# First attention of a two-block model: key panel first, compression links between attention steps, half-height masks and scores, two modulation vectors summed on GpSimd

## The chip, the cores and the metric

The kernel runs on one core of one Trainium2 chip. The metric is the device time of one execution in microseconds (us); three executions of the kernel before are shown below. TensorE is called PE, its weight loads PEld, VectorE DVE, ScalarE ACT, GpSimd POOL and SyncE SP. "The first attention" is the attention of the first layer; the times in this document are counted from the first instruction of the profiled execution.

## The reference, cut to what matters

A sequence of 256 tokens of width 1024 passes through four layers. Layer 0 is the one that is changed most:

```
mod = silu(c) @ ada_w[i] + ada_b[i]            # 6 vectors of 1024 per layer, 24 in all
h   = rms_norm(x, attn_norm) * (1 + sc) + sh
mq, mk, mv, nq, nkv, ng = split(h @ w_in)       # 512, 512, 512, 512, 768, 24 columns
o_moba = causal attention of 8 heads (64 wide) on norm+rope(mq), norm+rope(mk), mv
kc, vc = compress(kv[0,0]), compress(kv[0,1])   # 15 blocks of 32 tokens: silu(blocks @ w1) @ w2
o_nsa  = g0 * softmax(q kc) vc + g1 * causal attention(q, ks, vs) + g2 * causal attention(q, kw, vw)
x = x + g_a * (concat(o_moba, o_nsa) @ w_out);  x = x + g_f * swiglu(...)
```

With 256 tokens the selected blocks and the window of the reference cover every earlier token, so that all three of its full branches are plain causal attentions. Layer 1 has a causal attention with two maps per head, layer 2 a pooling, layer 3 a joint attention.

## The kernel before

**Projections.** Float32 products are made of three passes over a high and a low part: `L1508` (high weights, high activations), `L1509`, `L1510`. A weight arrives in units of two rows of 128 (a buffer `wraw` of four units, queue SP). ACT copies a unit to its high part `whi` (L526), DVE subtracts it to get the low part `wlo` (L903), and PE then multiplies; the split of unit u + 2 may start when unit u is done. `row_segment` does four such units and leaves a panel of rows in PSUM, which `panel_rows` copies to `work` (L597 on ACT, L955 on DVE). The projection of layer 0 is three panels in the order in0_0 (mq, mk; 1024 columns), in0_1 (mv, nq; 1024 columns), in0_2 (nkv and the gates; 792 columns). `head_norm` and `rotate` (L1059 to L1096, DVE) norm and rotate the heads of a panel while the next is multiplied; those of in0_2 have no next panel.

**Modulation vectors.** A vector of 1024 needs four ring units of 1 MB (two buffers `ring`, issued by ACT, L315). `vector_unit` multiplies each on PE (L1480: weights are columns of `cpad`, 32 wide, at four column positions), `vector_out` adds the bias on DVE (L866). `ada_step` places them between other work. Vectors 0 to 2 stand before and in in0_0, 3 and 4 in the compression, 5 in the first four attention steps. A vector is not needed before its norm or gate: 3 and 4 by the norm after out0, for which `columns(0, 1)` turns them.

**Between projection and attention.** `turns(0)` transposes 20 groups of heads (PE L1673, copies L655 on ACT and L1104 on DVE), DVE builds the compression's blocks (L1281), PE multiplies them with the compression weights (L1794, these too come through the ring), and a chain of small links follows: silu, transpose (L1800), second product (L1807, L1810), spreading (L1818), scores (L1825), softmax on DVE (L1299 to L1315), transpose (L1832), values (L1837), rows (L1319). PE, DVE and ACT take turns in it.

**Attention.** `attention(0)` has 12 steps of two heads. In step i PE does the scores of i, the transposes of i - 1 (L1723) and the values of i - 2 (L1742 to L1744); DVE takes the maxima of i (L1119 to L1121) and the rows of i - 2 (L1144 to L1163); ACT does the exponentials of i (L676) and copies the transposes of i - 1 (L690). For each head PE writes the causal mask as a product with the identity (L1705, 128 rows) and adds three score products of 64 rows (L1706 to L1708). `attention(1)` of layer 1 uses the same `scores`. Then come `out_turn(0)` (L1766), the output projection out0, the residual, the norm, and up0, whose first instruction is L1568.

The order on each engine is the order of its program; nothing is reordered by a scheduler. Waits are on semaphores, and an engine that waits holds everything behind it.

Of the kernel before, what the change touches and what calls it, by code (L numbers as in the profile page):

```python
# [7 lines left out]
F32 = mybir.dt.float32  # L8
# [7 lines left out]
P = 128  # L16
# [26 lines left out]
def shape_constants():  # L43
# [10 lines left out]
    put("causal", np.concatenate([causal, causal], 1))  # L54
# [37 lines left out]
def build(nc, x, c, positions, ada_w, ada_b, attn_norm, ffn_norm, ffn_w_gate, ffn_w_up, ffn_w_down,  # L92
# [6 lines left out]
    with stack:  # L99
# [25 lines left out]
        ident_r = sb("ident_r", [P, P], F32R)  # L125
        causal_r = sb("causal_r", [P, 2 * P], F32R)
# [26 lines left out]
        kcs = sb("kcs", [P, 32])  # L153
# [17 lines left out]
        T_BANKS = (6, 0, 1, 3)  # L171
        xn = wk(12288, 2048).rearrange("p (t n) -> p t n", t=TT)
# [8 lines left out]
        cmp_s = wk(14384, 256).rearrange("p (t h n) -> p t h n", t=TT, h=8)  # L181
        cmp_T = wk(14640, 256).rearrange("p (t n) -> p t n", t=TT)
        hidr = work[0:64, 14896:15152]
# [23 lines left out]
        for n, (a, b) in enumerate(((0, 1024), (1024, 2048), (2048, SP_IN))):  # L207
            seg(f"in0_{n}", "row", [SPI[:, :, a:b]], 4, b - a)
# [43 lines left out]

        tile0_done, quarter_done = sem("tile0_done"), sem("quarter_done")
# [15 lines left out]
        CMP_AT = 12  # L269
        RING_UNITS = 4 * VECTORS + 4  # L270
# [4 lines left out]
        def ring_at(g, j):  # L275

            return 4 * g + j + (0 if g < 3 else 4)

        def ring_unit(r):

            if CMP_AT <= r < CMP_AT + 4:
                return "cmp", (r - CMP_AT) // 2, (r - CMP_AT) % 2
            r -= 4 if r >= CMP_AT + 4 else 0
            return "ada", r // 4, r % 4


        STEP_PLAN = [g_ for g_ in range(VECTORS) if g_ < 6 or 9 <= g_ < 12 or g_ >= 21]
        STREAM_PLAN = {"up0": (6, 3), "up1": (12, 5), "down1": (17, 1), "up21": (18, 3)}
        EARLY = range(2, 8)
# [8 lines left out]
        def ring_dma(eng, r):  # L298
# [3 lines left out]
            kind, a, b = ring_unit(r)  # L302
# [4 lines left out]
            if kind == "ada":  # L307
                l, v = a // 6, a % 6
                at = v * D
                src = adaw[l][2 * b * P:(2 * b + 2) * P, :].rearrange("(k p) n -> p k n", p=P)[:, :, at:at + D]  # L310
                dst = dst.rearrange("p (k n) -> p k n", k=2)
            else:
                dst = dst.rearrange("p (k e) -> p k e", k=8)
                src = w1c[a][:, b * 8:(b + 1) * 8, :]
# [17 lines left out]
        PANEL_SEGS = ["in0_0", "in0_1", "in0_2", "out0", "down0", "in1_0", "in1_1", "in1_2", "out1", "down1",  # L332
# [15 lines left out]
        def q_groups(stage):  # L348

            if stage == 0:  # L350
# [7 lines left out]
                return [([src(r, t) for r in (2 * g, 2 * g + 1) for t in range(TT)], qt0[:, 2 * g:2 * g + 2, :]) for g in range(10)]  # L358
# [12 lines left out]
        def att(stage):  # L371
# [9 lines left out]
            a.ada = {0: 4, 1: 8, 3: 8}[stage]  # L381
# [14 lines left out]
        HEADS = [(0, 0), (0, 1), (0, 2), (1, 0), (1, 1), (3, 0), (3, 1), (3, 2)]  # L396
        head_squares = sem("head_squares")

        def heads_of(layer, n):

            if layer == 0:
# [7 lines left out]
                return views, HD, [wk(7728 + 1024 * t, 1024) for t in range(TT)], gains[:, lo:hi, :], n  # L409
# [16 lines left out]
        def _(sp):  # L426
# [14 lines left out]
            def weight_dma(s_, i):  # L441
                u = s_["base"] + i
                slot = u % 4
                if u >= 4:
                    sp.wait_ge(lo_ready, 2 * (u - 3))
                dst = wraw[:, slot, 0:unit_width(s_)].rearrange("p (k n) -> p k n", k=unit_split(s_))
                sp.dma_start(dst, unit_source(s_, i)).then_inc(raw_full[slot], 16)

            sp.wait_ge(ring_used, 4)
            for s_ in segs:  # L450
                if s_["name"] == "in0_1":
# [15 lines left out]
                    sp.dma_start(res[:, 1, :, :], ctx_2[0].rearrange("(t p) n -> p t n", p=P)).then_inc(sem("ctx_landed"), 16)  # L467
                for i in range(s_["count"]):
                    weight_dma(s_, i)
# [1467 lines left out]
```

## Time and profile before

| | |
|---|---|
| time of the three runs | 1750.68 us median (1749.74 to 1754.14) |
| span of the profiled execution | 1748.3 us, 2.4 us under the median; no other time of that execution is recorded |
| PE busy | 1575.0 us (90%) |
| PE weight loads busy | 1322.1 us (76%) |
| DVE busy | 940.4 us (54%) |
| ACT busy | 718.2 us (41%) |
| POOL busy | 0.2 us, 4 instructions |
| granted PE clock, mean | 0.940 |
| ACT split L526, mean of one | 1045 ns, two to a unit |
| DVE split L903, mean of one | 1216 ns, two to a unit |

The busy share of PE is an average over stages. In the stretches of in0 and of the attention steps PE is nearly always busy; between them it is not, and there its granted clock is lower as well. A stage is read by who waits for whom at its end.

### The profile page before, as it was taken

The numbers are of one execution on the slowest core, as the hardware profiler recorded it, in microseconds if no ns is written. First come the engines' busy times: TensorE is split into PE (matmuls) and PEld (weight loads), VectorE is DVE, ScalarE is ACT, GpSimd is POOL, SyncE is SP. The second block draws the span as 40 slices with busy tenths as digits, with TensorE's granted clock in tenths as the row PEclk, the third lists the DMA queues.
The fourth block names the chain that finished last, engine by engine and source line by source line (L and its number), as shares of the span: only waits on it lengthen the run. The fifth ranks groups of instructions, "written<-read, shape, count | busy, mean of one in ns | idle before, by whom it ended". The sixth has DMA issues, their size and how long they took to land.

```text
span 1748.3 us, 24466 instructions
## 1 busy us (share of the span) xinstructions
PE 1575.0 (90%) x10302; PEld 1322.1 (76%) x10302; DVE 940.4 (54%) x1610; ACT 718.2 (41%) x1098; POOL 0.2 (0%) x4
## 2 busy tenths in 40 slices
PE   3966988999989888999988999889999795999997
PEld 1753677999868657999768998679987673779986
DVE  2591346434577776433566345663355786364455
ACT  1441244334445434333335554354544443345543
POOL 0000000000000000000000000000000000000000
PEclk9988798999989889999988999889999897989999
DMA  9844602985545546998753645549755353436452
GB/s 359 313 149 158 224 19 79 315 286 188 174 147 185 176 142 214 307 307 302 242 180 97 190 172 193 181 137 300 249 185 202 109 181 109 162 129 192 169 192 85
DMA packets 165845, 336.42 MB, mean 192 GB/s; under 512 B 8160, under 2 KB 109160, under 8 KB 165480
## 3 DMA queue, kind: packets, MB, share of 16 engines
q1 hardware_dynamic: 134720, 226.71, 38.0%
q10 hardware_dynamic: 31016, 108.16, 18.2%
q8 instruction: 81, 1.33, 0.3%
q14 instruction: 28, 0.23, 0.0%
HBM read 333.79 MB, written 1.05 MB: 192 GB/s over the span
## 4 chain that ended last, share of the span: by engine, by line
PE 80%; DVE 13%; DMA 2%; ACT 2%; issue 1%; ACTq 0%; SPq 0%; DVEq 0%
PE ps L1508 21%; PE ps L1509 21%; PE ps L1510 20%; PE ps L1480 5%; DVE wlo L903 3%; PE ps L1639 2%; DVE res L981 1%; DVE work L979 1%; PE ps L1636 1%; PE ps L1723 1%; PE ps L1673 1%; PE ps L1706 1%; DMA ring<-in_ada_w_dram 1%; PE ps L1702 1%; DVE work L1066 1%
## 5 line engine op out<-in xcount | busy, mean ns | idle before, releaser
L903 DVE TENSOR_TENSOR wlo<-wraw,whi 128x1024 fp32r<-128x1024 f32 (+1 forms) x424 | 497.9, 1216 | 404.4 <-ACT whi L526 403.9
L526 ACT ACTIVATE whi<-wraw 128x1024 fp32r<-128x1024 f32 (+1 forms) x424 | 423.1, 1045 | 468.7 <-PE ps L1510 447.0
L1508 PE MATMUL ps<-hT_hi,whi 128*128 128x256 f32 x1472 | 422.5, 287 | 0.0
L1509 PE MATMUL ps<-hT_lo,whi 128*128 128x256 f32 x1472 | 416.9, 283 | 0.0
L1510 PE MATMUL ps<-hT_hi,wlo 128*128 128x256 f32 x1472 | 416.5, 283 | 0.0
L1508 PEld LDWEIGHTS ps<-hT_hi,whi 128*128 128x128 f32 x1472 | 282.7, 192 | 20.3 <-issue 18.1
L1509 PEld LDWEIGHTS ps<-hT_lo,whi 128*128 128x128 f32 x1472 | 282.9, 192 | 0.0
L1510 PEld LDWEIGHTS ps<-hT_hi,wlo 128*128 128x128 f32 x1472 | 282.8, 192 | 0.0
L1508 PE MATMUL ps<-whi,act_hi 128*128 128x512 f32 x560 | 219.0, 391 | 0.0
L1509 PE MATMUL ps<-wlo,act_hi 128*128 128x512 f32 x560 | 218.1, 390 | 0.0
L1510 PE MATMUL ps<-whi,act_lo 128*128 128x512 f32 x560 | 217.9, 389 | 0.0
L1508 PE MATMUL ps<-whi,hT_hi 128*128 128x512 f32 (+2 forms) x416 | 161.8, 389 | 7.8 <-DVE hT_lo L1030 7.4
L1509 PE MATMUL ps<-wlo,hT_hi 128*128 128x512 f32 (+2 forms) x416 | 158.9, 382 | 0.0
L1510 PE MATMUL ps<-whi,hT_lo 128*128 128x512 f32 (+2 forms) x416 | 158.2, 380 | 0.0
L897 DVE TENSOR_TENSOR act_lo<-work,act_hi 128x512 fp32r<-128x512 f32 x70 | 48.4, 692 | 191.8 <-ACT whi L526 191.8
L1508 PEld LDWEIGHTS ps<-whi,act_hi 128*128 128x128 f32 x560 | 105.1, 188 | 25.6 <-issue 3.8
L522 ACT ACTIVATE act_hi<-work 128x512 fp32r<-128x512 f32 x70 | 44.1, 630 | 191.4 <-issue 170.2
L1510 PEld LDWEIGHTS ps<-whi,act_lo 128*128 128x128 f32 x560 | 105.1, 188 | 21.9
L1509 PEld LDWEIGHTS ps<-wlo,act_hi 128*128 128x128 f32 x560 | 105.1, 188 | 21.6
L1480 PE MATMUL ps<-ring,cpad 128*32 128x256 f32 x1440 | 103.4, 408 | 11.0 <-DMA ring<-in_ada_w_dram 10.3
L1508 PEld LDWEIGHTS ps<-whi,hT_hi 128*128 128x128 f32 x416 | 79.5, 191 | 28.7 <-DVE hT_lo L1030 8.3
L1510 PEld LDWEIGHTS ps<-whi,hT_lo 128*128 128x128 f32 x416 | 79.2, 190 | 15.1
(200 smaller groups left out, 1372.1 us busy)
## 6 DMA issues: line engine op xcount, KB each, us to landing
wraw<-in_mlp_w_dram SPq DMA_DIRECT2D x96, 1024.0 KB, 5.3
ring<-in_ada_w_dram ACTq DMA_DIRECT2D x90, 1024.0 KB, 5.3
wraw<-in_ffn_w_gate_dram SPq DMA_DIRECT2D x22, 1024.0 KB, 6.4
wraw<-in_ffn_w_up_dram SPq DMA_DIRECT2D x22, 1024.0 KB, 5.6
wraw<-in_ffn_w_down_dram SPq DMA_DIRECT2D x22, 1024.0 KB, 4.9
wraw<-in_diff_w_in_dram SPq DMA_DIRECT2D x12, 1024.0 KB, 4.9
wraw<-in_attn_w_qkv_dram SPq DMA_DIRECT2D x12, 1024.0 KB, 5.1
wraw<-in_sp_w_in_dram SPq DMA_DIRECT2D x8, 1024.0 KB, 13.0
```

The lines of the kernel that those rows point to most:

```text
L522: nc.scalar.activation(act_hi[:, u % 2, :], hid[:, at:at + 512], ACT.Copy)
L526: nc.scalar.activation(whi[:, u % 2, part], wraw[:, u % 4, part], ACT.Copy).then_inc(hi_ready, 1)
L897: nc.vector.tensor_tensor(act_lo[:, u % 2, :], hid[:, at:at + 512], act_hi[:, u % 2, :].bitcast(F32), ALU.subtract)
L903: nc.vector.tensor_tensor(wlo[:, u % 2, part], wraw[:, u % 4, part], whi[:, u % 2, part].bitcast(F32), ALU.subtract).then_inc(lo_ready, 1)
L979: nc.vector.tensor_tensor(tmp[:, t, cols], ps[:, D_BANKS[q], :], gate_b[:, cols], ALU.mult).then_inc(dve_emptied, 1)
L981: nc.vector.tensor_tensor(res[:, strm, t, cols], res[:, strm, t, cols], tmp[:, t, cols], ALU.add).then_inc(sem("res_ready"), 1)
L1066: return nc.vector.tensor_tensor(views[t], views[t], g.rearrange("p a (c d) -> p a c d", c=1).to_broadcast([P, a, b, width]), ALU.mult)
L1480: ins = mm(ps[32 * c_:32 * c_ + 32, ADA_BANK, 0:256], cpad[:, 0 if g < 12 else 1, kt, :], ring_view(r)[:, kk * D + 256 * c_:kk * D + 256 * ...
L1508: mm(dst, s_hi, m_hi, start=start, stop=False, skip_group_check=skip)
L1509: mm(dst, s_hi, m_lo, start=False, stop=False, skip_group_check=skip)
L1510: return mm(dst, s_lo, m_hi, start=False, stop=stop, skip_group_check=skip)
L1639: ins = nc.tensor.transpose(ps[:, T_BANKS[b], (k % 2) * S + t * P:(k % 2) * S + (t + 1) * P], xn[:, t, k * P:(k + 1) * P], ident)
```

## The change

Four things are changed, all before up0 except the score order in layer 1.

1. **Panel order.** in0_2 is multiplied first, then in0_0, then in0_1. Key heads are normed during in0_0, MoBA heads during in0_1, and only the eight NSA query heads after the last panel. The splits of the first two units of out0 move from the end of in0 into attention steps 8 and 10 (`own=True`).
2. **Compression links.** The compression weights come through `wraw` on the SP queue, their products alternate between two column positions, and the links from the first transpose on stand one by one behind attention steps 0 to 12, in PSUM bank 7. `ada_step` leaves the compression and the attention.
3. **Scores.** The mask is two products of 64 rows per head, and masks and scores alternate between the two heads, whose operands lie in partitions 0 to 63 and 64 to 127. In layer 0 and layer 1.
4. **POOL.** Vectors 3 and 4 are summed by POOL: per ring unit two row blocks, each multiplied by a column of `cpad` and added up (30 instructions of 128x1024), and PE only folds the 128 partitions (`sum_fold`). Vector 5 stands in out0. The load of `ctx_2` moves behind the eighth unit of up0, since its buffer holds the sums.

```diff
@@ scores(i), PE, stages 0 and 1
-                        mm(ps[:, bank, 0:256], ident_r[:, :], causal_r[:, :], start=True, stop=False, skip_group_check=True)
-                        mm(ps[:, bank, 0:128], q[:, 0:128], k[:, 0:128], start=False, stop=True, skip_group_check=True)
...
+                        for half in range(2):
+                            for m in range(2):
+                                lo, hi = HD * m, HD * m + HD
+                                bank = 2 * (i % 2) + m
+                                mm(ps[:, bank, 0:256], half_r[lo:hi, HD - HD * half:3 * HD - HD * half], causal_r[lo:hi, half, :, :].rearrange("p b n -> p (b n)"),
+                                   start=(half == 0), stop=False, skip_group_check=True)
+                        for tq, tk, at in ((0, 0, 0), (1, 1, 128), (1, 0, 256)):
+                            for m in range(2):
...
+                                ins = mm(ps[:, bank, at:at + P], q[:, tq * P:(tq + 1) * P], k[:, tk * P:(tk + 1) * P], start=False, stop=True, skip_group_check=True)
@@ PE, main program
-            for n in range(3):
-                row_segment(f"in0_{n}", ada=(n == 0))
+            row_segment("in0_2", ada=True)
+            row_segment("in0_0")
+            row_segment("in0_1")
+            pe.wait_ge(sem("doubled"), 1)
+            turns(0, 0, 4)
+            pe.wait_ge(sem("moba_heads0"), 1)
+            turns(0, 4, 8)
             gate()
...
+            attention(0, beside=compression)
+            pe.wait_ge(sem("cmp_taken"), 2)
+            sum_fold(0)
+            out_turn(0)
+            sum_fold(1)
+            row_segment("out0", ada=True)
             columns(0, 1, 6)
-            out_turn(0)
-            row_segment("out0")
@@ DVE, main program
+            row_segment("in0_1", heads=lambda i: heads0(0, (i,)), own=True)
+            nc.vector.memset(mark[:, 1:2], 0.0).then_inc(sem("moba_heads0"), 1)
+            panel_rows(r0, 1024, 1024)
+            turns(0, 0, 4)
...
+            heads0(1, (0, 1))
+            turns(0, 4, 6)
+            heads0(1, (2,))
+            turns(0, 6, 8)
+            heads0(1, (3,))
+            nc.vector.memset(mark[:, 1:2], 0.0).then_inc(sem("query_heads0"), 1)
@@ ACT, beside the panels and the steps
+            def summed_ring(i):
+                if i % 2:
+                    ring_fill(ring_at(3, 0) + 2 + (i + 1) // 2)
...
+                if i in (8, 10):
+                    split_unit(by_name["out0"]["base"] + (i - 8) // 2)
@@ POOL, new
+            def row_sum(g, acc):
+                for j in range(4):
+                    r = ring_at(g, j)
+                    ring_wait(pool, r)
+                    for kk in range(2):
...
+                            link(nc.gpsimd.tensor_scalar(w, w, cpad[:, 0, kt, 0:1], None, ALU.mult))
+                            ins = nc.gpsimd.tensor_tensor(acc, acc, w, ALU.add)
...
+                    ins.then_inc(ring_used, 1)
```

PE, from the end of the projection to the first attention step; `cst` holds the identity, L1480 is a modulation unit. Before:

```order
L1659 MATMUL ps<-modrow,cst 128x256 x4
L1673 MATMUL ps<-cst,work 128x128 x40
L1794 MATMUL ps<-ring,work 30x256 x32
L1480 MATMUL ps<-ring,cpad 32x256 x8
L1800 MATMUL ps<-cst,work 128x64 x2
L1480 MATMUL ps<-ring,cpad 32x256 x8
L1807 MATMUL ps<-hbuf,w2k 128x30 x2
L1810 MATMUL ps<-w2v,hbuf 15x64 x4
L1480 MATMUL ps<-ring,cpad 32x256 x8
L1818 MATMUL ps<-vcr,cst 128x64 x8
```

The same place now; L1863 are the half masks and L1869 the scores of the first step:

```order
L1826 MATMUL ps<-cst,work 128x128 x32
L1807 MATMUL ps<-modrow,cst 128x256 x4
L1958 MATMUL ps<-wraw,work 30x256 x32
L1826 MATMUL ps<-cst,work 128x128 x8
L1863 MATMUL ps<-causal_r,half_r 128x256 x4
L1869 MATMUL ps<-work 128x128 x6
L1969 MATMUL ps<-cst,work 128x64 x2
L1863 MATMUL ps<-causal_r,half_r 128x256 x4
```

Eight of ten transpose groups stand before the compression product, two behind it, then the steps begin at once; the links are between them.

DVE, behind the last panel of the projection, now: the panel's copy (L1017), the turns' copies (L1166), the blocks of the compression (L1355), then the norm of the query heads:

```order
L1340 MEMSET mark 128x1
L1017 COPY work<-ps 128x512 x2
L1166 COPY work<-ps 128x512 x2
L1355 TENSOR_TENSOR work<-work,paramT 64x8x15 x16
L1357 MEMSET work 64x256
L1358 MEMSET work 128x256
L1121 TENSOR_REDUCE stat<-work 128x8 x2
L1136 TENSOR_SCALAR stat<-stat 128x16
```

Before, this norm stood between the panels, and that of the key heads in its place, ahead of all transposes.

POOL, new, one ring unit of vector 3 (`res` is the sum):

```order
L1567 TENSOR_SCALAR res<-ring,cpad 128x1024
L1569 TENSOR_SCALAR ring<-ring,cpad 128x1024
L1570 TENSOR_TENSOR res<-res,ring 128x1024
L1569 TENSOR_SCALAR ring<-ring,cpad 128x1024
L1570 TENSOR_TENSOR res<-res,ring 128x1024
```

Each addition is a read of two operands in SBUF, as is DVE's split L903.

## Rows read from the trace of the kernel before

**Rows 1.** Windows: start:end, length, busy us (instructions) per engine, clock, DMA.
```profile
112.00:198.00 86.00, 53.55 (x316) 30.47 (x315) 31.94 (x100) 14.97 (x30) 0.00 (x0) 0.70 0.47 160
175.00:198.00 23.00, 19.87 (x135) 10.90 (x135) 6.84 (x20) 1.70 (x2) 0.00 (x0) 0.54 0.67 229
220.00:250.00 30.00, 30.00 (x226) 26.51 (x224) 16.27 (x57) 16.79 (x64) 0.00 (x0) 1.00 0.02 8
```
**Rows 2.** Waits of PE from 40 to 262 us: total, times, longest.
```profile
PE ps L1673 <- ACT work L744: 10.6, 1, 10.6
PE ps L1480 <- DMA ring<-in_ada_w_dram: 10.3, 4, 5.4
PE ps L1794 <- DVE work L1281: 5.7, 1, 5.7
```
**Rows 3.** Timeline of PE, projection: start, duration, engine, line, operands.
```profile
45.36 0.80 PE L1508 MATMUL ps<-whi,hT_hi 128*128 128x512 f32 x1 [7.02 <-DVE hT_lo L1030]
52.80 1.07 PE L1480 MATMUL ps<-ring,cpad 128*32 128x256 f32 x16
59.51 1.07 PE L1480 MATMUL ps<-ring,cpad 128*32 128x256 f32 x16
94.59 0.39 PE L1508 MATMUL ps<-whi,hT_hi 128*128 128x512 f32 x1
95.27 0.29 PE L1508 MATMUL ps<-whi,hT_hi 128*128 128x280 f32 x1
95.65 0.39 PE L1508 MATMUL ps<-whi,hT_hi 128*128 128x512 f32 x1
112.65 0.29 PE L1510 MATMUL ps<-whi,hT_lo 128*128 128x280 f32 x1
```
**Rows 4.** Timeline of DVE, projection and behind it.
```profile
82.56 2.34 DVE L1059 TENSOR_REDUCE stat<-work 128x16 f32<-128x1024 f32 x2 [0.58 <-ACT work L575]
85.46 2.36 DVE L903 TENSOR_TENSOR wlo<-wraw,whi 128x1024 fp32r<-128x1024 f32 x2 [0.56 <-ACT whi L526]
87.74 0.17 DVE L1074 TENSOR_SCALAR stat<-stat 128x32 f32<-128x32 f32 x1
90.50 1.23 DVE L1063 TENSOR_TENSOR work<-work,rstat 128x1024 f32<-128x1024 f32 x1
137.21 4.59 DVE L1281 TENSOR_TENSOR work<-work,paramT 64x120 f32<-64x120 f32 x16
```
**Rows 5.** Timeline of PE, one attention step of layer 0 and the next step's start.
```profile
224.58 0.36 PE L1705 MATMUL ps<-causal_r,ident_r 128*128 128x256 f32 x1
226.91 0.87 PE L1723 MATMUL ps<-cst,work 128*128 128x128 f32 x6
228.88 0.36 PE L1705 MATMUL ps<-causal_r,ident_r 128*128 128x256 f32 x1
```
**Rows 6.** Timelines of DVE and ACT in that step.
```profile
227.02 0.43 DVE L1119 TENSOR_REDUCE rowmax<-ps 128x2 f32<-128x256 f32 x1 [1.51 <-PE ps L1708]
228.28 0.37 ACT L676 ACTIVATE work<-ps,rowmax 128x128 f32<-128x128 f32 x1 [1.88 <-DVE rowmax L1121]
229.11 0.18 DVE L1144 RECIPROCAL coef<-rowsum 128x4 f32<-128x4 f32 x1 [0.86 <-PE ps L1744]
229.88 0.82 ACT L690 ACTIVATE work<-ps 128x768 f32<-128x768 f32 x1
230.04 0.49 DVE L1163 TENSOR_TENSOR work<-work,hbuf 128x128 f32<-128x128 f32 x2
```
**Rows 7.** Timeline of PE, compression and modulation, in order of time.
```profile
142.05 8.38 PE L1794 MATMUL ps<-ring,work 128*30 128x256 f32 x32 [5.67 <-DVE work L1281]
174.35 3.67 PE L1818 MATMUL ps<-vcr,cst 15*128 15x64 f32 x16
```
**Rows 8.** Timeline of PE behind the attention.
```profile
260.99 1.12 PE L1497 MATMUL ps<-cst,modrow 128*128 128x128 f32 x4 [1.58 <-DVE work L1163]
297.92 0.57 PE L1568 MATMUL ps<-zero 1*128 1x512 bf16 x1
```
**Rows 9.** Waits of DVE in layer 1's attention, 603 to 622 us.
```profile
DVE rowmax L1119 <- PE ps L1708: 1.9, 4, 0.9
```

More of the change, by code:

```diff
@@ L746, in _ @@
+            row_segment("in0_1", heads=(0, 0), beside=doubled_keys, own=True)
+            panel_rows(r0, 1024, 1024)
+            next_panel()
+            turns(0, 0, 2)
+            square_heads(0, 1)
+            turns(0, 2, 8)
             gate()
-            turns(0)
-            c0 = CMP_AT
-            ring_fill(c0 + 4)
-            act.wait_ge(ring_used, c0 + 4)
+            act.wait_ge(cmp_used, 2)
             act.wait_ge(sem("hidr_zero"), 1)
             for s_ in range(2):
-                ins = nc.scalar.activation(hidr[32 * s_:32 * s_ + 30, :], ps[32 * s_:32 * s_ + 30, 0, 0:256], ACT.Silu)
+                ins = nc.scalar.activation(hidr[32 * s_:32 * s_ + 30, :], ps[32 * s_:32 * s_ + 30, LINK_BANK, 0:256], ACT.Silu)
@@ L1097, in rotate, with turns @@
                 link(ins)
-            def turns(stage):
-                for g, (_, dst) in enumerate(q_groups(stage)):
+            def turns(stage, first=0, last=None):
+                for g, (_, dst) in list(enumerate(q_groups(stage)))[first:last]:
                     if g % 2 == 1:
@@ L1323, in _ @@
+            attention(0, beside=compression)
+            vector_out(3)
+            out_turn(0)
+            vector_out(4)
+            row_segment("out0", ada=True)
+            residual(0)
             columns(0, 1)
-            out_turn(0)
-            row_segment("out0")
-            residual(0)
             norm()
@@ L1665, in gate, with turns @@
                     gate_out[0] = (gate_copied, 2 * sum(1 for g in GATES[:e + 1] if not (g[0] == 2 and g[2] == 0)))
-            def turns(stage):
-                for g, (srcs, _) in enumerate(q_groups(stage)):
+            def turns(stage, first=0, last=None):
+                groups = q_groups(stage)
+                last = len(groups) if last is None else last
+                for g in range(first, last):
+                    srcs, _ = groups[g]
                     if g >= 4:
@@ L1842, in _ @@
+            attention(0, beside=compression)
+            pe.wait_ge(sem("cmp_taken"), 2)
+            sum_fold(0)
+            out_turn(0)
+            sum_fold(1)
+            row_segment("out0", ada=True)
             columns(0, 1, 6)
-            out_turn(0)
-            row_segment("out0")
             gate()
```

494 lines of the change are left out of this document (297 added, 197 removed).

## The prediction

> **What bounds the kernel now.** I read the windows by stage first. In the attention steps PE is busy all of the 30 us at full clock, but in the 86 us between the last panel (112 us) and the first step (198 us) it is busy 53.6 us at a mean clock of 0.70, and at 0.54 in the last 23 us [rows 1]. Then the waits of PE: 10.6 us for the doubled keys behind the last head norm, 10.3 us for four ring units, 5.7 us for the blocks [rows 2]. Third, the timelines. The projection runs from 45.4 to 112.9 us [rows 3]. An attention step is 4.30 us (224.58 to 228.88), all PE: 2.33 for masks and scores (to 226.91), 1.97 for transposes and values [rows 5]. So the stretch of links is bound by latency, and the steps by PE. From the attention's last row (260.9) to up0 (297.9) are 37.0 us [rows 8]. I therefore sum the way to up0, and treat the rest as unchanged but for layer 1.
>
> **Projection.** One group of three matmuls costs 0.68 us 512 wide and 0.38 us 280 wide (94.59, 95.27, 95.65) [rows 3]. A 1024 unit has eight wide groups, 5.44 us; a 792 unit four of each, 4.24 us. The first unit cost 7.44 us (45.36 to 52.80), 2.0 over that, and a modulation unit between adds 1.27 (59.51 - 52.80 - 5.44) [rows 3]. The narrow panel is first now, so a unit lands and is split sooner: splits are proportional to width, (1 - 792/1024) x (1.05 + 2.36) = 0.8 us, and about 1 us I estimate for the landing of 0.2 MB less. Start 45.4 - 1.8 = 43.6. in0_2: 4 x 4.24 + 2.0 + 3 x 1.27 = 22.8, to 66.4. in0_0 and in0_1: 8 x 5.44 = 43.5, to 109.9. The panels in sum are the same work; 3 us come from the start and from a stall-free end. The ring needs 1 MB more often here (every 5.5 us beside 0.8 MB of weights); I leave up to 3 us for that in the range.
>
> **What DVE has left when in0_1 ends.** In in0_1 it splits unit 2 and 3 and norms 32 heads. in0_1 starts at 88.1; the split of its unit 2 opens when unit 0 is done: 93.6, plus 1.05 ACT and 2.36 DVE, 97.0; the two totals 2.34, 99.4. Unit 3 opens at 99.0 and is split at 102.4; the chain of small ones until L1063 took 2.76 (87.74 to 90.50) [rows 4], then four passes of 1.2 and a rotation of 2.8: 112.8. So DVE is 2.9 us behind PE even alone.
>
> **POOL's price.** No POOL arithmetic is in the trace. One of its 128x1024 instructions costs at least what DVE needs, 1.18 us (half of 2.36), and at most what the dearest row per element gives: 16 adds of 120 elements in 4.59 us are 2.4 ns an element, so 2.45 us [rows 4]. I take 1.7: 30 of them are 51 us, spread by the ring from 65 to about 160 us; PE wants the sums at 207 and later. Hidden, unless an instruction costs over about 4.5 us. What is not hidden is that DVE may have to wait for POOL. Before, POOL is idle, so the trace excludes neither nothing nor everything: the eight instructions of the ring units that land around 100 and 105 us fall on the head norms of in0_1, where each microsecond of DVE is on the path: 0 to 14 us. I take 6, somewhat under half, since the totals, copies and PSUM operations between read one SBUF operand.
> The Trainium skill, SBUF — State Buffer, section Who interferes with whom, says that a DVE instruction with two SBUF inputs and a GpSimd one that reads SBUF exclude each other for a whole instruction. By that rule alone, with every POOL instruction in the way, the term would be 14 us instead of 6. The Trainium skill, GPSIMD Engine Reference, section Elementwise — side-by-side cycle accounting, gives 4497 ns for an addition of 2048 elements, from which I estimate 2.2 us for 1024. No run here shows either yet.
>
> **From there to the first step.** DVE starts at 112.8 + 6 = 118.8: panel copies 1.3, turns' copies with a wait 2.1, blocks 4.6 [rows 4], two fills 0.5, query heads (half as wide: totals 1.3, chain 2.6, four passes 2.8, rotation 2.0), two copies 1.4, gates 0.7, last turns 1.1: 20.4 us. PE's own way fits under it if the 32 compression products, now at two column positions, run in pairs: each is two passes, of 0.22 to 0.26 us (8.38 us for 32 passes) [rows 7], so the 64 passes are 14 to 16 us one after the other and 7 to 8 in pairs. That column positions overlap the trace shows: L1480, 16 passes at four positions, takes 1.07 us [rows 3], where 16 in series at 0.22 would take 3.5. So the first step starts at 139.2 instead of 197.6.
>
> **The steps.** PE's part for masks and scores can fall from 2.33 to 0.9 us if the 64-row products of two heads overlap, and stay near 2.1 if they don't (then only the changes between 128 and 64 rows go). I take 1.5. But then PE is not the bound: maxima to exponentials 1.26 (227.02 to 228.28), exponentials 1.60 (to 229.88), row operations until 1.42 after 229.11 [rows 6]: a step would be 3.4 to 3.6 us. Into this go the links: on PE some 6 us (spreading L1818 3.67 at half clock is 1.8 [rows 7]), in steps 1 to 3 each with a round trip PE to DVE and back, in steps 4 and 5 1.5 and 2.0 us of softmax ahead of the next maxima, in 8 and 10 a split of 2.36 ahead of them. Going through 14 rounds with these durations I get 63.6 us (62.3 with scores at 1.2, 65.8 at 1.9). The same reckoning gives 60.4 for before, where 63.3 were measured, so 3 us are added, and 1.3 for an activation table that was loaded under cover before. 67.9: the attention gains nothing by itself, its scores pay for the links. It ends at 207.1 instead of 260.9.
>
> **Behind it.** out0 now holds vector 5: 4 x 1.0 = 4.0, two folds 0.4 us: 37.0 + 4.4 = 41.4. up0 starts at 248.5 instead of 297.9: 49.4 gained. In layer 1 the faster scores find DVE the bound: it waited 1.9 us in four steps for them [rows 9], so eight steps give about 2.4. Sum 51.8. 1748.3 - 51.8 = 1696.5 span, and 2.4 more for the median of the runs: **1698.9**.
>
> **Rivals.**
> A. **POOL and DVE do not meet**, rows overlap fully, PE feeds the steps at once. The 6 us of contention go, 1.3 for scores at 1.2, and the 3 us added to the steps: 1688.6. For it: only two of eight ring units fall on DVE's tight stretch. Against: DVE's work there is nearly all two-operand. 0.20.
> B. **A latency takes the place of the waits.** DVE pays the full 14 us (8 more), and the steps, now with PE pausing 1 to 2 us in each, are granted half clock for a part: PE's 38 us of work in them at a mean of 0.85, which I choose between those 0.70 and 1, cost nearly 7 more. 1713.6. For it: clock 0.54 to 0.70 in the stretches with pauses [rows 1]. 0.22.
> C. **Heads one after the other.** Scores stay near 2.1 to 2.3, links then come on top: by the same rounds 67.2 to 69.3 instead of 63.6, and layer 1 gives nothing: 6 to 8 us more, 1706. Inside the range. 0.10.
> D. **POOL is the bound, and the kernel is slower.** ACT waits in its own order for `ring_used` before it issues the next ring unit, with the splits behind it, and PE waits for the second sum at 208. The sums are through at 65 + 30 p. At p = 6.5 us that is 260, which eats the 52 us; the blocked splits of in0_0 begin to cost already from p = 3.6 (three instructions by 76 us). So 5 to 6 us an instruction decide, four times DVE's 1.18. At 6.5 the second sum is 53 us late, which is the time of before, and the blocked ring adds about 10: 1760. 0.03.
> The forecast's own case has the remaining 0.45.
> The Trainium skill, TensorE: Matmul & The Clock Gate, section Packing small matmuls, says that small row tiles run concurrently; by it C would be out. No row of before shows it for rows.
>
> **Numbers.** 0.3% (5 us) is about what a measurement of this kernel can tell from no change. All cases but D are faster by more; between them and D lies a thin case in which several terms fail: faster 0.95, same 0.02, slower 0.03. The range goes from 1685 (A with 3 us more from the projection) to 1715 (B): 8 in 10.
>
> **What would show it.** First step of the attention (first L1863) at 139, between 131 and 148; attention 68 us long, its steps 3.4 to 3.7 us where no link stands; up0's first product near 248; POOL instructions of 1.2 to 2.5 us, done by 165, and L964 (the split) longer than 1.18 where POOL works; layer 1's step 4.2 instead of 4.5. It would be wrong if in0_0 or in0_1 stall for the ring or for splits, if POOL instructions pass 4 us, or if the pauses in the steps pull the clock down.

## The result, and the profile after

The changed kernel takes **1727.0 us** (median of 4 runs, 1724.2 to 1732.3) against 1752.4 us before: a ratio of 0.986, 95% interval 0.984 to 0.988. It is faster by 1.4%, about half of the 3% that was forecast, and 28 us above the forecast of 1698.9, outside its range. Its profiled execution is the longest of the four (1732.3 us, span 1730.5), so stretches of its trace add up to some 34 us over the forecast span of 1696.5, and medians to 28. The kernel before was run again beside each group of experiments (medians 1752.6, 1750.7 and 1750.9 us), so differences between runs of different groups are uncertain by about 2 us.

The timeline of PE has the landmarks that the prediction named (start, duration, engine, line, operands): a modulation unit and the last products of the first panel, the link of the turns behind the panels, the first step, the end of the attention, the first product of up0, and a step of layer 1.

```profile
50.65 1.07 PE L1616 MATMUL ps<-ring,cpad 128*32 128x256 f32 x16
67.00 0.29 PE L1646 MATMUL ps<-whi,hT_lo 128*128 128x280 f32 x1
...
121.13 1.47 PE L1826 MATMUL ps<-cst,work 128*128 128x128 f32 x12
...
155.01 0.79 PE L1863 MATMUL ps<-causal_r,half_r 64*128 64x256 f32 x4 [0.90 <-ACT work L692]
238.43 1.08 PE L1700 MATMUL ps<-res,fold 128*32 128x256 f32 x8 [1.52 <-DVE work L1231]
281.97 0.60 PE L1716 MATMUL ps<-zero 1*128 1x512 bf16 x1
...
593.67 0.51 PE L1863 MATMUL ps<-causal_r,half_r 64*128 64x256 f32 x4
594.01 0.83 PE L1869 MATMUL ps<-work 64*128 64x128 f32 x12
594.77 0.55 PE L1884 MATMUL ps<-cst,work 128*128 128x128 f32 x3
```

The first panel ends at 67.1 us, as forecast (66.4). The other two end at 121.1 instead of 109.9, the first step comes at 155.0 instead of 139.2, the attention takes 83.4 us instead of 67.9, and up0 starts at 282.0 instead of 248.5 (before: 297.9 [rows 8]). What is left of the gain at that point is 15.9 us, and the span gains 17.8. Layer 1's attention is 1.7 us shorter (39.7 instead of 41.3); the last 0.2 is what is left of small shifts elsewhere, 1.4 us lost ahead of it and 1.6 won behind it.

The waits of PE from 44 to 155 us answer to [rows 2]. The doubled keys and the blocks are gone from them; the longest wait is now for VectorE's copy of the last panel (left out here are 5.7 us ahead of the first product, where it was 7.0 before, and one of 1.0):

```profile
PE ps L1826 <- DVE work L1017: 13.3, 1, 13.3
PE ps L1644 <- DVE wlo L964: 6.1, 5, 3.3
PE ps L1826 <- DVE mark L1364: 3.2, 1, 3.2
```

Windows by stage (length; busy us of PE, PEld, DVE, ACT, POOL with instructions; PE's granted clock; DMA share, GB/s), which answer to [rows 1]:

```profile
88.00:112.00 24.00, 19.11 (x73) 14.37 (x72) 23.79 (x27) 12.40 (x21) 23.36 (x8) 0.93 0.56 183
112.00:135.00 23.00, 8.44 (x41) 6.28 (x39) 22.34 (x34) 2.55 (x8) 22.40 (x9) 0.83 0.40 133
155.00:175.00 20.00, 17.54 (x120) 16.29 (x121) 5.43 (x17) 7.17 (x27) 10.75 (x5) 0.59 0.49 175
175.00:197.00 22.00, 20.61 (x116) 19.67 (x116) 7.88 (x26) 7.68 (x28) 10.13 (x5) 0.50 0.00 0
197.00:217.00 20.00, 15.91 (x150) 13.98 (x147) 12.74 (x39) 12.53 (x44) 0.00 (x0) 0.93 0.49 157
217.00:238.40 21.40, 17.66 (x82) 15.42 (x80) 10.18 (x33) 6.59 (x17) 0.00 (x0) 0.50 0.16 51
```

Two things stand out. From 88 to 135 us DVE and POOL are both busy nearly all the time, and PE in 27.6 of 47 us. And the attention, which ran at full clock before in 30 us of it [rows 1] and in the 22 ahead of them, is granted 0.50 to 0.59 for its first 42 us and 0.50 again for its last 21. The timelines of DVE and POOL, side by side in the first of these stretches, show what the first is:

```profile
87.60 2.63 DVE L1125 TENSOR_TENSOR work<-work,rstat 128x384 f32<-128x384 f32 x1
93.34 2.72 DVE L1125 TENSOR_TENSOR work<-work,rstat 128x384 f32<-128x384 f32 x1
95.98 0.55 DVE L1128 TENSOR_TENSOR work<-work,gains 128x384 f32<-128x384 f32 x1
100.03 2.77 DVE L1128 TENSOR_TENSOR work<-work,gains 128x384 f32<-128x384 f32 x1
```

```profile
87.43 2.38 POOL L1570 TENSOR_TENSOR res<-res,ring 128x1024 f32<-128x1024 f32 x1
89.91 3.03 POOL L1569 TENSOR_SCALAR ring<-ring,cpad 128x1024 f32<-128x1024 f32 x1
93.02 2.62 POOL L1570 TENSOR_TENSOR res<-res,ring 128x1024 f32<-128x1024 f32 x1
95.74 3.42 POOL L1569 TENSOR_SCALAR ring<-ring,cpad 128x1024 f32<-128x1024 f32 x1
99.24 3.13 POOL L1570 TENSOR_TENSOR res<-res,ring 128x1024 f32<-128x1024 f32 x1
```

A DVE instruction that takes 0.55 us by itself takes 2.6 to 2.8 when it starts just behind one of POOL: POOL's sum of 87.43 ends at 89.81, and DVE's product of 87.60 at 90.23, 0.42 later; 93.02 ends at 95.64, DVE's at 96.06; 99.24 ends at 102.37, DVE's at 102.80. DVE is held for the rest of POOL's instruction and then does its work. It happens the other way round too: DVE's product of 95.98 runs its 0.55 us, and POOL's of 95.74, beside it, takes 3.42 instead of the 2.85 that it takes alone. The Trainium skill, SBUF — State Buffer, section Who interferes with whom, says that a DVE instruction with two SBUF inputs contends with a GpSimd one that reads SBUF, and calls the shared ports an exclusive lock. The trace agrees.

### The profile page after: what moved, and what is told of

Read it like the earlier page. It is cut to its first block, busy times and chain, and to the rows that moved or that the text cites. A ratio compares the mean times of both kernels' runs of the same rounds, so it can differ in the third digit from the quotient of the medians.

```text
span 1730.5 us, 24335 instructions
## 1 busy us (share of the span) xinstructions
PE 1554.7 (90%) x10214; PEld 1317.9 (76%) x10214; DVE 963.3 (56%) x1612; ACT 718.7 (42%) x1098; POOL 89.7 (5%) x36
## 3 DMA queue, kind: packets, MB, share of 16 engines
q10 hardware_dynamic: 26856, 103.96, 17.8%
## 4 chain that ended last, share of the span: by engine, by line
PE 77%; DVE 16%; ACT 2%; issue 2%; DMA 2%; ACTq 0%; SPq 0%; DVEq 0%
PE ps L1644 22%; PE ps L1645 21%; PE ps L1646 21%; PE ps L1616 4%; DVE wlo L964 3%; PE ps L1787 2%; DVE res L1043 1%; DVE work L1041 1%; PE ps L1884 1%; PE ps L1784 1%; DVE work L1128 1%; DVE work L1125 1%; PE ps L1857 1%; ACT whi L561 1%; PE ps L1896 1%
## 5 line engine op out<-in xcount | busy, mean ns | idle before, releaser
L964 DVE TENSOR_TENSOR wlo<-wraw,whi 128x1024 fp32r<-128x1024 f32 (+1 forms) x424 | 505.3, 1233 | 408.7 <-ACT whi L561 408.1
L1644 PEld LDWEIGHTS ps<-hT_hi,whi 128*128 128x128 f32 x1472 | 282.1, 192 | 20.2 <-issue 18.1
L1616 PE MATMUL ps<-ring,cpad 128*32 128x256 f32 x1312 | 88.7, 389 | 3.2 <-DVE modrow L927 1.4
```

The costliest lines, as they stand in the source:

```text
L964: nc.vector.tensor_tensor(wlo[:, u % 2, part], raw_view(u)[:, part], whi[:, u % 2, part].bitcast(F32), ALU.subtract).then_inc(lo_ready, 1)
L1616: ins = mm(ps[32 * c_:32 * c_ + 32, ADA_BANK, 0:256], cpad[:, 0 if g < 12 else 1, kt, :], ring_view(r)[:, kk * D + 256 * c_:kk * D + 256 * ...
L1644: mm(dst, s_hi, m_hi, start=start, stop=False, skip_group_check=skip)
```

## The experiments

Theory P: GpSimd holds VectorE back by its instructions, mostly ahead of the first step. Theory R: the links between the steps, with their pauses, take the clock away, and this makes the attention long. Rivals: the ring, released late by GpSimd, is what costs (to P); the half clock comes from the overlapping half-height products, or from what lies ahead of the attention (to R); the links cost by their own work.

### First: take POOL's work away, and undo the scores

**e1_pool_two_ops**, GpSimd's work reduced:

```diff
-    link(nc.gpsimd.tensor_scalar(w, w, cpad[:, 0, kt, 0:1], None, ALU.mult))
-    ins = nc.gpsimd.tensor_tensor(acc, acc, w, ALU.add)
+    ins = nc.gpsimd.tensor_scalar(w[:, 0:1], w[:, 0:1], cpad[:, 0, kt, 0:1], None, ALU.mult)
```

> Changed kernel, but POOL does one full 128x1024 multiplication per vector and otherwise one-column instructions (the sums are left out, so vectors 3 and 4 are not those of the reference); all else stands. Theory P (POOL holds VectorE's operands back): VectorE comes to the last panel's copy about 113 us instead of 134.6, the first attention step at about 134 instead of 155.0, time about 20 us under the changed kernel, 1706 us. Rival Q (VectorE is late by its own order of work, and POOL only runs beside it): first step still near 155, time within 5 us of 1727. Rival R (POOL's instructions are what keeps the clock of the attention low): the attention, 83.4 us now, comes down to about 68 as well, 1691 us.

Measured: 1705.3 us (1702.4 to 1706.6), ratio 0.973 [0.971, 0.975]; 21.7 us under the changed kernel. The panels end at 109.9 us and the first step comes at 134.0 (forecast without contention: 109.9 and 133.2). The attention still takes 78.9 us. So P holds, and it is nearly all ahead of the first step: 21.0 us there in the traces, 4.5 in the steps (by the medians 21.7 in all). Windows from the second panel's start to the first step, and over the attention, first of the changed kernel, then of this run:

```profile
67.13:155.01 87.88, 63.20 (x307) 47.55 (x305) 80.38 (x141) 31.17 (x49) 68.64 (x23) 0.90 0.55 199
155.01:238.43 83.42, 71.72 (x461) 65.36 (x461) 36.24 (x113) 33.97 (x114) 20.87 (x9) 0.62 0.28 93
```

```profile
66.33:133.98 67.65, 59.23 (x306) 45.82 (x305) 56.74 (x141) 31.13 (x49) 14.36 (x13) 0.97 0.69 253
133.98:212.87 78.89, 63.27 (x460) 57.87 (x460) 35.93 (x113) 33.81 (x114) 1.23 (x5) 0.74 0.29 97
```

Ahead of the first step, the same 141 instructions of VectorE take 23.6 us less, and its idle time grows by 3.4 (from 7.5 to 10.9): together the 20.2 us by which the stretch is shorter. A ring that is released late would have to show as idle time of VectorE in the changed kernel, and there is less of it there, not more (ScalarE waits once for GpSimd, 4.5 us, and VectorE is busy throughout that wait). So the ring has no visible share. In the attention VectorE's instructions take 36.2 us against 35.9: the lock costs next to nothing there, and the 4.5 us go with the clock, 0.62 against 0.74 in the mean.

**e2_vectors_on_pe**, both vectors back on TensorE, in the two panels that have no units now, and POOL idle:

```diff
-STEP_PLAN = [0, 1, 2, 5, 9, 10, 11, 21, 22, 23]
-POOL_PLAN = (3, 4)
+STEP_PLAN = [0, 1, 2, 3, 4, 5, 9, 10, 11, 21, 22, 23]
+POOL_PLAN = ()
...
-            row_segment("in0_0")
-            row_segment("in0_1")
+            row_segment("in0_0", ada=True)
+            row_segment("in0_1", ada=True)
```

> Changed kernel with POOL idle: vectors 3 and 4 are modulation units on TensorE again, four beside in0_0 and four beside in0_1, no folds. Theory P: the projection grows by 8 x 1.27 = 10 us on TensorE, of which 3 lie under VectorE's lateness, and the 22 us of held VectorE work go: first attention step at about 142 instead of 155, one to two us less behind the attention; time about 1712 if the attention stays at 83 us, about 1700 if its clock comes back. Rival Q (no contention): the 7 us are added and nothing is given back, 1733 us.

Measured: 1711.9 us (1711.4 to 1712.2), ratio 0.977 [0.975, 0.978]. The eight units cost TensorE 7.6 us (first step at 141.6 against 134.0; 6.6 by the medians), about a third of what it costs to have GpSimd do them. The attention takes 78.0 us, with POOL idle throughout: its length is a matter of its own.

**e3_old_scores**, the changed kernel with the old masks and scores (full-height mask product, heads one after the other):

```diff
-for half in range(2):
-    for m in range(2):
-        mm(ps[:, bank, 0:256], half_r[lo:hi, ...], causal_r[lo:hi, half, :, :]...)
+for m in range(2):
+    mm(ps[:, bank, 0:256], ident_r[:, :], causal_o[:, :], start=True, ...)
```

> Changed kernel with the score order of before in both attentions (one 128-row mask a head, heads one after the other). Theory C (the 64-row products that overlap keep the granted clock at its lower level, as the array is filled by fewer instructions): the attention's clock comes back to near 1 from 0.53 to 0.59, a step gets the longer scores but at full clock, the attention is 5 to 10 us shorter than 83.4, layer 1's is 2 us longer; time 1719 to 1724. Rival D (the pauses of the links keep the clock low, whatever the scores): every step is longer by the scores at half clock, 2.0 to about 4.5 us, the attention by 15 to 25 us, time about 1750.

Measured: 1762.7 us (1762.1 to 1766.1), ratio 1.006 [1.005, 1.008]: slower than before. The attention takes 110.3 us (154.3 to 264.5). Its windows:

```profile
154.00:174.00 20.00, 19.71 (x80) 16.39 (x80) 4.00 (x11) 7.25 (x27) 8.54 (x4) 0.50 0.38 129
174.00:194.00 20.00, 17.23 (x73) 15.61 (x72) 4.46 (x13) 2.56 (x10) 12.29 (x6) 0.50 0.11 45
194.00:214.00 20.00, 20.00 (x82) 17.54 (x82) 7.98 (x26) 5.66 (x22) 0.00 (x0) 0.50 0.00 1
214.00:234.00 20.00, 20.00 (x84) 17.93 (x83) 5.99 (x20) 8.70 (x28) 0.00 (x0) 0.50 0.30 99
```

The clock is at half here too, with no overlapping products, so these don't bring it down. At half clock the dense steps are bound by PE, and the old scores of one head take 2.06 us where they take 1.15 at full clock: 35.7 us over the changed kernel by the medians (29.8 in the traces, 26.9 of them in this attention). I hadn't expected the half clock to last these 80 us (154 to 234), with PE busy in 96% of them; why it does not rise there I can't say.

**e4_scores_only**, the kernel before with nothing but the new masks and scores (the same code as above, the other way):

> Kernel before with the new score order alone, in both attentions. If row positions overlap, masks and scores take 1.1 us instead of 2.33 a step at full clock; a step of layer 0 is then bound by the way over VectorE and ScalarE, 3.3 us instead of 4.3 (12 us over twelve steps), and layer 1 gives 2: 1738 us. If the new products pull the clock down even in a dense attention (theory C), the gain is gone in layer 0: 1748 us or above, with a granted clock under 0.8 in its steps.

Measured: 1739.0 us (1738.1 to 1743.1), ratio 0.993 [0.991, 0.995]. The attention takes 54.2 us instead of 63.4, at a clock of 1.00 in two thirds of it. With no links between the steps the clock is as high as before, and the half-height products save their time in it and, by some 2 us, in layer 1.

### Second: what POOL does, and what the links do

**f1_pool_memsets**, GpSimd busy without reading:

```diff
-    link(nc.gpsimd.tensor_scalar(w, w, cpad[:, 0, kt, 0:1], None, ALU.mult))
-    ins = nc.gpsimd.tensor_tensor(acc, acc, w, ALU.add)
+    link(nc.gpsimd.memset(w, 0.0))
+    link(nc.gpsimd.memset(w, 0.0))
+    ins = nc.gpsimd.memset(w, 0.0)
```

> The changed kernel, with GpSimd's products and sums of the two modulation vectors replaced by memsets of the same 128x1024 tiles (two vectors then hold zeros, so the adaptive scales and shifts of one sublayer are wrong). GpSimd stays busy in the same stretch and frees the ring about as late, but reads nothing from SBUF. If it is the reading of SBUF by GpSimd that holds VectorE back, the time is that of the kernel with the sums cut to one column: about 1705 us (1703 to 1708). If any busy GpSimd, or the late release of the ring, is what costs, it stays near the changed kernel's 1727 us (1720 to 1730).

Measured: 1701.9 us (1700.5 to 1709.5), ratio 0.973 [0.971, 0.975]. The memsets are shorter than the arithmetic (0.95 us each, 42 us in sum instead of 89), so the ring comes free earlier than I meant it to, and this run alone doesn't exclude the ring (VectorE's idle time, above, does). But where they overlap, VectorE shows nothing of them: its 141 instructions ahead of the first step take 55.8 us, no more than the 56.7 of e1_pool_two_ops, with GpSimd busy for 30.7 us beside them. Rows of DVE and of POOL in this run:

```profile
86.00 0.55 DVE L1125 TENSOR_TENSOR work<-work,rstat 128x384 f32<-128x384 f32 x1
86.47 0.55 DVE L1128 TENSOR_TENSOR work<-work,gains 128x384 f32<-128x384 f32 x1
```

```profile
85.12 0.95 POOL L1571 MEMSET ring<- 128x1024 f32 x1
86.14 0.95 POOL L1569 MEMSET ring<- 128x1024 f32 x1
```

The Trainium skill, in the same section of SBUF — State Buffer, limits the block to GpSimd instructions that read SBUF; these two rows agree.

**f2_fillers**, extra matmuls beside the links (on e2_vectors_on_pe):

```diff
 def compression(i):
+    if i < 5:
+        for _ in range(8):
+            mm(ps[:, 2 * ((i + 1) % 2), 0:256], half_r[0:HD, HD:3 * HD], causal_r[0:HD, 0, :, :]..., start=True, stop=True)
```

> The version with all vectors on TensorE (1711.9 us), with eight extra matmuls (64x256) ahead of each of the first five places between steps, where TensorE otherwise waits for the link's answer; they write a score bank that the next step overwrites. If the half clock of the first attention is due to the pauses beside the links, the clock returns and the attention shrinks from 78.0 to about 70 us: about 1704 us. If the fillers only cost their own time (40 of 0.13 us at full clock, 0.20 at half, less the 5 us of waits they lie in), the time is 1712 to 1716 us.

Measured: 1712.4 us, but its four runs are 1704.5, 1716.4, 1708.4 and 1718.2, a spread of 13.7 us that no other kernel here has. The profiled run is the first. Its attention is 69.8 us (141.4 to 211.2), and the clock in it:

```profile
141.00:160.00 19.00, 17.03 (x169) 15.57 (x169) 7.74 (x24) 9.82 (x36) 0.00 (x0) 1.00 0.31 126
160.00:180.00 20.00, 18.06 (x189) 16.96 (x189) 11.93 (x40) 10.26 (x38) 0.00 (x0) 1.00 0.01 2
180.00:200.00 20.00, 16.32 (x116) 13.90 (x115) 13.06 (x36) 12.26 (x38) 0.00 (x0) 0.78 0.24 68
```

In this run more work on PE made the stretch 8 us shorter, as R has it. The other three runs left no trace, but each has its mean granted clock on record: 0.945 in the profiled run, and 0.943, 0.940 and 0.937 in those of 1708.4, 1716.4 and 1718.2 us. The longer the run, the lower its clock; where in the run it fell is not shown. As a remedy fillers are no good.

**f3_no_links**, the links left out on all engines (on e2_vectors_on_pe):

```diff
 def compression(i):
+    return
```

> The version with all vectors on TensorE (1711.9 us), with the compression's links left out of the first attention on all engines (its part of the output is missing). If the links with their pauses hold the clock down, the twelve steps run as in the kernel with the new scores alone (54.2 us with its clock at 1.00 in two thirds of it): the attention takes about 54 us instead of 78.0, and the time is about 1688 us. If the clock is low for another reason (what comes ahead of it, or the steps themselves), only the links' own 12 us of work and 4 us of waits go: about 62 us, 1696 us or more.

Measured: 1694.8 us (1693.1 to 1698.0), ratio 0.968 [0.967, 0.970]. The attention takes 61.0 us: between the two expectations and nearer the second. The clock is 0.91 to 1.00 until 180 us and 0.57 behind it. The links with all they bring cost 17.1 us (with some 2 us of uncertainty between the groups), and a part of the low clock, at the end, isn't theirs.

**f4_links_spaced**, the links two and three steps apart (on e2_vectors_on_pe; TensorE's side, VectorE's and ScalarE's moved likewise):

```diff
-                if i == 1:
+                if i == 2:
                     pe.wait_ge(sem("cmp_hidT_sb"), 1)
...
-                if i == 2:
+                if i == 4:
                     pe.wait_ge(sem("cmp_kv_sb"), 1)
...
-                if i == 3:
+                if i == 6:
                     pe.wait_ge(sem("cmp_vbd"), 1)
...
-                if i in (9, 11):
+                if i in (11, 12):
```

> The version with all vectors on TensorE (1711.9 us), with the links set two and three steps apart (TensorE's at steps 0, 2, 4, 6, 9, 11, 12; VectorE's answers at 1, 3, 5, 7 and 8, 10, 12, 13), so that each answer has a step to be ready in. If the pauses of the links hold the clock down, the 4 to 5 us of waits go and the clock rises: attention about 70 us, the time about 1704 us. If the clock stays at half, only the waits go, less one new wait at the end: 1708 to 1711 us.

Measured: **1694.7 us** (1693.8 to 1695.7), ratio 0.968 [0.967, 0.970]: better than either expectation, and level with the run that has no links at all. The attention takes 62.4 us. Windows, and a link without its wait (in e2_vectors_on_pe the same 16 products take 3.67 us, behind a wait of 1.4):

```profile
140.60:160.00 19.40, 16.68 (x167) 15.55 (x168) 8.52 (x28) 11.91 (x45) 0.00 (x0) 0.91 0.28 113
160.00:180.00 20.00, 17.79 (x173) 16.66 (x172) 10.93 (x38) 9.98 (x38) 0.00 (x0) 0.91 0.00 1
180.00:205.00 25.00, 16.25 (x134) 14.20 (x135) 17.14 (x49) 12.96 (x35) 0.00 (x0) 0.97 0.28 86
```

```profile
158.52 1.99 PE L1980 MATMUL ps<-vcr,cst 15*128 15x64 f32 x16
```

The same instructions on the same engines, in other steps: 17.2 us by the medians of two groups, 15 by their ratios. Windows over the attention, first of e2_vectors_on_pe, then of this run:

```profile
141.56:219.60 78.04, 61.91 (x460) 56.49 (x461) 35.85 (x113) 33.81 (x114) 0.00 (x0) 0.75 0.16 57
140.62:203.05 62.43, 48.77 (x461) 44.44 (x461) 35.99 (x113) 33.64 (x114) 0.00 (x0) 0.95 0.20 69
```

PE's same matmuls take 13.1 of the 15.6 us less, and busy time times clock is the same (46.4 and 46.3 us): they are done at a higher clock. Its idle time falls by only 2.5 us, since the two waits for links, 1.4 each, are gone and two new ones of 2.4 and 2.5 stand at the end. The mean clock of all four runs agrees (0.949 to 0.951, against 0.940). So it is shown that spacing the links brings the clock back. That short pauses are what takes it away is not: PE waits about as long in both, and in f3_no_links, with no link at all, the mean clock of the attention is 0.82.

### Third: put together, and where else GpSimd could work

**g1_after_spaced**: the whole changed kernel with the links moved as in f4_links_spaced.

> The changed kernel whole (GpSimd's sums and all), with the links set two and three steps apart as in the version that took 1694.7 us. If GpSimd's hold on VectorE and the links' pauses are two separate losses, the attention shrinks from 83.4 us by as much as it did there (78.0 to 62.4), and the time is about 1710 us (1706 to 1713). If GpSimd's work inside the attention is what keeps the clock low or VectorE late there, the spacing gives little: 1718 us or more.

Measured: 1715.2 us (1711.7 to 1718.9), ratio 0.980 [0.977, 0.982]: 11.8 us under the changed kernel, between the two. In the traces the attention goes from 83.4 to 65.4 us and the span from 1730.5 to 1710.8, but the two profiled runs lie at opposite ends of their kernels' runs. The two losses are mostly separate. Some of the gain is lost where both are present: the attention is 3.0 us longer than the 62.4 of f4_links_spaced, and VectorE's same 113 instructions take 3.6 us more in it (39.6 against 36.0), with single scalings of 128x4 held up to 2.06 us. From 155 to 175 us PE is granted 1.00 here and 0.59 in the changed kernel, though it waits longer here (4.0 us against 3.4): the length of the pauses alone doesn't set the clock.

**g2_tail**, the last two waits of f4_links_spaced out of the way:

```diff
-                    else:
-                        pe.wait_ge(sem("cmp_taken"), 1)
-                    mm(ps[:, LINK_BANK, :], cmp_T[:, t, :], vbd, ...)
+                    mm(ps[:, (LINK_BANK, 1)[t], :], cmp_T[:, t, :], vbd, ...)
...
 def out_turn(stage):
     for b in range(4):
+        if stage == 0 and b == 2:
+            pe.wait_ge(ATT[0].taken, 12)
+            pe.wait_ge(sem("cmp_taken"), 2)
```

> The version with spaced links (1694.7 us) with its last two waits taken out: the compression's second product goes to a score bank of its own, so that it doesn't wait for VectorE to read the first (2.4 us), and the first half of the output's transposes, which reads only columns that are complete, goes ahead of the wait for the last steps (2.5 us). If these waits lie on the path, 1690 to 1692 us; if VectorE's last additions set the end either way, 1693 to 1695 us.

Measured: **1688.5 us** (1686.5 to 1691.5), ratio 0.964 [0.962, 0.966], the best version with the reference's full work: 3.6% under the kernel before and 38.5 us under the changed one. It gives 6.2 us by the medians (3.0 by the spans of the two profiled runs) for 4.9 us of waits; one wait of 1.57 us is left at that place.

**g3_late_sums**, one vector summed by GpSimd while the attention runs (on f4_links_spaced; the ring's loads move with it):

```diff
-STEP_PLAN = [0, 1, 2, 3, 4, 5, 9, 10, 11, 21, 22, 23]
-POOL_PLAN = ()
+STEP_PLAN = [0, 1, 2, 3, 5, 9, 10, 11, 21, 22, 23]
+POOL_PLAN = (4,)
...
+            pool.wait_ge(ATT[0].scores, 1)
```

> The version with spaced links (1694.7 us), with one of the two vectors (the fifth) summed by GpSimd while the attention runs, started by its first score, instead of by TensorE in the third key panel. If GpSimd costs by the large VectorE instructions that it meets there, few of which read two operands from SBUF in the attention, the panel's four units of TensorE work are won (3.8 us, half of the 7.6 between the first steps of the two versions measured) and little is lost: about 1691 us (1689 to 1693). If GpSimd's instructions cost about the same wherever they lie (22 us for 32 of them, so 11 us for 16), it is about 1702 us.

Measured: 1702.6 us (1698.0 to 1704.1), ratio 0.971 [0.970, 0.973]: the second expectation. The first step comes 1.7 us earlier (139.0 against 140.6), and the attention takes 73.1 us instead of 62.4. The groups of DVE in it (instructions | busy, mean ns) show a lock that I had not looked for there. With GpSimd:

```profile
L1176 DVE TENSOR_REDUCE rowmax<-ps 128x2 f32<-128x512 f32 x12 | 8.1, 678 | 0.0
L1177 DVE TENSOR_SCALAR rowmax<-rowmax 128x4 f32<-128x4 f32 x12 | 6.3, 527 | 0.4
```

and without it, in f4_links_spaced:

```profile
L1181 DVE TENSOR_REDUCE rowmax<-ps 128x2 f32<-128x512 f32 x12 | 8.2, 680 | 0.0
L1182 DVE TENSOR_SCALAR rowmax<-rowmax 128x4 f32<-128x4 f32 x12 | 2.0, 171 | 0.4
```

What reads PSUM is untouched. The scaling of four maxima, 0.17 us of work on the way from every score to its exponentials, is held until GpSimd's instruction ends. One pair, DVE and POOL:

```profile
151.98 1.88 DVE L1177 TENSOR_SCALAR rowmax<-rowmax 128x4 f32<-128x4 f32 x1
```

```profile
151.48 2.35 POOL L1563 TENSOR_TENSOR res<-res,ring 128x1024 f32<-128x1024 f32 x1
```

The one ends at 153.86, the other at 153.83. The twelve cost 4.3 us more in sum, and all of VectorE's instructions in the attention 5.5 (41.5 against 36.0). But PE's idle time grows by 1.0 us only, and its busy time by 9.7 (58.5 against 48.8): most of the 10.7 us is clock, 0.78 to 0.85 instead of 0.91 to 0.97. That the lock is what lowers the clock is likely and not shown. (GpSimd's work in the changed kernel was 30 such instructions, not the 32 of the expectation; here it is 15.)

**g4_tail_late_sums**: both edits.

> Both edits of this call on the version with spaced links: if they are independent, the sum of their two differences, about 1688 us.

Measured: 1696.6 us (1693.8 to 1697.5), ratio 0.968 [0.967, 0.970]. As the first edit gave -6.2 and the second +7.9, their sum is 1696.4: independent. The 1688 that was expected rested on the first expectation for g3_late_sums, which failed.

## Why the prediction was wrong

The direction was right (faster, 0.95) and the range was not. By its steps, in the profiled executions, where 34.0 us are to be explained:

- **Projection: right.** The first panel ended at 67.1 (66.4), and without GpSimd's work the other two ended at 109.9 (109.9).
- **"I take 6": the step that failed first.** The first step came 15.8 us late, and e1_pool_two_ops brought it to 134.0, so the term is 21.0 us instead of 6, above the upper bound of 14. Three parts of it were wrong. The price: GpSimd's instructions take 2.35 (sum) and 2.85 us (product) undisturbed, not 1.7; my upper bound of 2.45 lay under the commoner of them. The spread: at that price GpSimd doesn't follow the ring, it works without a break from 67 to 138 us, so 22 of the 30 instructions lie beside VectorE's work there and not eight. And what can be hit: I counted the norms' large passes of in0_1, but the splits (L964, mean 1.70 us in 65 to 135 us, 1.23 in e1_pool_two_ops) and small operations are held too, and with the splits the panels themselves, 11.2 us by their end. The condition "hidden, unless an instruction costs over about 4.5 us" was true of GpSimd's own deadline and said nothing of the engine beside it. The Trainium skill's rule that I had weighed (SBUF — State Buffer, Who interferes with whom) was right about the mechanism; its 14 us were bounded by my count of eight, and that was the error. The estimate from the Trainium skill, GPSIMD Engine Reference, section Elementwise — side-by-side cycle accounting, was 2.2 us for a sum, and a sum takes 2.35: it was nearer than my 1.7.
- **The 20.4 us from VectorE's last norm to the first step: right.** 134.6 to 155.0.
- **"67.9": the second step that failed.** Measured 83.4, 15.5 more. The rounds were worked out with PE's durations at full clock, and that is the wrong part: the mean clock of the attention was 0.62. With the links two or three steps apart and GpSimd idle it is 0.95, and the attention takes 62.4. Rival B had a low clock at "a mean of 0.85 cost nearly 7 more", worked out on 38 us of PE's work, which left out the links' 6: busy time times clock is 46 us. The trace shows 0.50 to 0.59 for 42 us, and f4_links_spaced puts the cost of the links' places at 15.6 us of the attention, 2.5 of them PE's idle time and 13.1 clock. Where I wrote "in steps 1 to 3 each with a round trip PE to DVE and back" I had named the places, and priced only the length of the waits.
- **Behind the attention: right within about 2.** 43.5 for 41.4. **Layer 1: right.** 1.7 for 2.4.
- **Masks and scores: right.** 1.10 us (593.67 to 594.77) where it was 2.33 [rows 5], at the low end of "0.9 to 2.1"; C is refuted. "The attention gains nothing by itself, its scores pay for the links" understated them: alone they bring 13.6 us by e4_scores_only (11.7 in the traces), and in the changed kernel, at half clock, 35.7 (29.8).
- **Rivals.** What happened is B, its first term half as large again (21 instead of 14) and its second double (15.5 instead of 7). That g2_tail comes to A's 1688.6 and e3_old_scores to D's 1760 is chance: they are other kernels and got there by other ways.

Open: what sets the granted clock in the attention. The clock stays at half in stretches where PE is busy throughout (e3_old_scores, and 182 to 197 us here), it is 0.62 in the changed kernel and 0.74 without GpSimd's work although the lock costs 0.3 us there, it is higher when the links are spaced although PE waits nearly as long, and it differs between runs of one kernel (f2_fillers).

## What to carry to other kernels

Before giving GpSimd arithmetic "beside" VectorE, list every VectorE instruction in the stretch that reads two operands from SBUF, or is a small scaling on a critical chain, and take up to one whole GpSimd instruction of waiting for each in the range; here 30 instructions of "free" work put off the first step by 21.0 us, and the same work on TensorE by 7.6. Where a chain of links is put between steps, give each answer a step to arrive in before anyone waits for it: it brought 15.6 us here, 13.1 of them through the clock of the steps around. And where a change puts new waits into a dense stretch, don't take its clock from the kernel before: work the sum out at both levels and put both in the range.

## What the runs showed of the hardware

- GpSimd: a product with a column operand (128x1024, float32) takes 2.85 us, a sum of two such tiles 2.35, a memset 0.95, when nothing disturbs them. The one-input form is the dearer one.
- VectorE's lock reaches down to the smallest instructions: 128x4 scalings with 0.17 us of work take up to 1.88 us in g3_late_sums and 2.06 in g1_after_spaced. Reciprocals of the same size (0.18 us on the mean of 11 in the attention of g3_late_sums), reductions and copies from PSUM are not held, and memsets by GpSimd hold nothing. The lock works both ways: GpSimd's product takes 3.42 instead of 2.85 where VectorE's of 0.55 comes between.
- Half-height products of two heads overlap: masks and scores of a step take 1.10 us (layer 1 of the changed kernel) instead of 2.33.
- The same matmuls in the same order but for the places of a few links took 61.9 us at a mean granted clock of 0.75 and 48.8 at 0.95 (e2_vectors_on_pe, f4_links_spaced).
- A clock that had fallen stayed at 0.50 for 80 us with PE busy in 96% of them (e3_old_scores); the kernel before had 1.00 in its steps from 198 to 250 us.
